# Rounding the next filter's weights at step 7 instead of 15, and building the attention bias ahead of the stores

## The chip, the cores and the metric

The kernel runs on one core of one Trainium2 chip. The metric is the device time of one execution in microseconds. The median of three runs before the change is 1096.94 us (1096.89 to 1097.17).

## The reference, cut to what matters

One layer of a hybrid encoder over 272 positions (256 tokens and 16 meta tokens) of width 2048. One input projection feeds three mixers, each gated, and their sum goes through an output projection:

```
z = rmsnorm(h) @ w_in                       # 2048 -> 16384 columns, split into the blocks below
u, x1, x2 = split(short_conv(hy_in))
kf  = rfft(filter from sin-MLP @ w4 * exp(-t * |decay|))     # hyena filter, 2 orders, two directions
y_a = hyena(u, x1, x2, kf) * silu(hy_gate)
y_b = real(fft2(fn_in)) * silu(fn_gate)
s   = q @ k.T * scale + bias(rpb) (masked) ; y_c = softmax(s) @ v * silu(na_gate)
m   = g_a * (y_a @ w_a) + g_b * (y_b @ w_b) + g_c * (y_c @ w_c)
out = rmsnorm(h + m @ w_out)[16:]
```

## The kernel before, in words

**Arithmetic.** Every float32 matrix product is made of three matmuls on split operands: a high part (the value rounded to the format that TensorE takes) and a low part (what is left). ScalarE makes the high part (`w_hi`, `act.split`, line 1016) and VectorE the low part by a subtraction (`w_lo`, `lo_part`, line 1359). GpSimd makes the low part of the filter weights `w4` for the first filter of chunks 1 to 3 (line 554).

**Chunks and steps.** The mixers' channels are cut into four chunks of 256 (`c` = 0 to 3). A chunk has 20 steps (`t`), and each step multiplies one slab of projection weights (48 matmuls, some 6 us) on TensorE. A block of columns takes two steps: u 0 and 1, q 2 and 3, k 4 and 5, v 6 and 7, x1 8 and 9, x2 10 and 11, the hyena gate 12 and 13, the Fourier input 14 and 15, then the other two gates. Between slabs TensorE does the mixers' smaller products. The slab of step `t + 2` is split during step `t`. A chunk takes 146 us, and the rows of chunks 0, 1 and 2 are 146.02 us apart to 0.02 us around the places in question.

**Order.** Each engine has its own list of instructions, written out by hand, in which a step's position is fixed; semaphores hold an instruction until its inputs are there. An engine never goes past an instruction that waits. What matters here:

- step 7, ScalarE and VectorE: after the softmax of head 0 (ScalarE's `soft`, VectorE's `normalized`, line 1709, which counts `p_done`) the first half of a slab is split, then VectorE copies block v out of PSUM (line 1595), which counts `proj_read`;
- step 8, TensorE: after its slab it turns the probabilities of head 0 (`turn_p`, lines 751 and 753, waits for `p_done`), and then v (`turn`, line 701, waits for `proj_read`);
- step 13, VectorE: the softmax of head 3. `biased` counts `smax_done` (line 1703), the slab is split, and `normalized` counts `p_done`;
- step 14, TensorE: after its slab, `attend(2)` and then `turn_p` of head 3, which waits for that `p_done`;
- step 15: ScalarE and VectorE finish the output of head 3 (`attended`, lines 1211 and 1721, `o_done`); TensorE's inverse transform waits for `o_done` at its second half (line 728, matmuls of line 717). VectorE's list has `fin_mirrors` (lines 1572 to 1574) ahead of `attended`.

**The filter.** `weights4(b)` on ScalarE rounds the weights `w4s` into `w4_hi` (line 1076) and takes the absolute value of `absd` (line 1078). When `w4_hi` is there, GpSimd subtracts to get `w4_lo` (line 554). The first user of the two is `make_h4` at step 16. GpSimd issues the loads of `w4s` and `absd` as soon as the filter before is no longer needed (`load_filter`, from step 2 on).

**GpSimd's list in a chunk:** load the next bias rows, load the next filter, `w4_lo`, store y_a, store y_c, load a filter, store y_b, and build the bias of the next chunk (`make_bias`: four additions of 128x384 at line 528, one for each head, and two copies at line 530).

Of the kernel before, what the change touches and what calls it, by code (L numbers as in the profile page):

```python
# [46 lines left out]
HC = HEADS // CH  # L47
# [146 lines left out]
def build(nc, x, meta, w_stream, filt_in, sym_in, fch_in, ftok_in, net_in, negt_in, mask_in, ident_in, params_in, w4,  # L194
# [138 lines left out]
    with ExitStack() as ctx:  # L333
        ps = ctx.enter_context(nc.psum_tensor("ps", [128, 8, 512], F32))

        def sem(name):
            return ctx.enter_context(nc.semaphore(name))
# [64 lines left out]
        smax_done = sem("smax_done")  # L402
# [72 lines left out]
        def _(pool):  # L475
# [9 lines left out]
            def load_filter(g):  # L485
                if g:
                    pool.wait_ge(h4_mm, 3 * g)
                    pool.wait_ge(env_done, 3 * g)
                for rows in (slice(0, HID), slice(HID, 2 * HID)):
                    pool.dma_start(w4s[rows, :, :].rearrange("p d n -> p (d n)"), w4[g]).then_inc(w4_landed, 16)  # L490
                pool.dma_start(absd[:, :, :].rearrange("p d n -> p (d n)"),
                               decay[g].partition_broadcast(128)).then_inc(dec_landed, 16)
# [20 lines left out]
            def load_bias_rows(c):  # L513
                for s in range(2):
                    src = bass.AP(rpb.tensor, c * (HC * RPB_R * RPB_C) + ((5 - s) * RPB_C + KW - GRID_W),
                                  [[1, GRID_W], [RPB_R * RPB_C, HC], [1, RPB_W]])
                    pool.dma_start(rows_t[64 * s:64 * s + 64, :, :], src).then_inc(b_landed, 16)
                pool.dma_start(meta_t[:, :], mbias[bass.ds(c, 1), :].rearrange("a n -> (a n)").partition_broadcast(128)
                               ).then_inc(b_landed, 16)

            def make_bias(c):
                pool.wait_ge(b_landed, (c + 1) * 48)
                for hh in range(HC):
                    grid = bias_t[:, hh, NM:NM + 6 * GRID_W].rearrange("p (j k) -> p j k", j=6)
                    flat = rows_t[:, hh, :]
                    toeplitz = bass.AP(flat.tensor, flat.offset, [[flat.ap[0][0], 128], [RPB_C, 6], [1, GRID_W]])
                    msk = mask[:, :].rearrange("p (a k) -> p a k", a=1).broadcast_to([128, 6, GRID_W])
                    nc.gpsimd.tensor_tensor(grid, toeplitz, msk, ALU.add)
                for lo in (0, NM + 6 * GRID_W):
                    last = nc.gpsimd.tensor_copy(bias_t[:, :, lo:lo + NM], meta_t[:, :].rearrange("p (h m) -> p h m", h=HC))  # L530
                last.then_inc(b_ready, 1)

            def store_y(c, branch, done):
                pool.wait_ge(done, c + 1)
                pool.dma_start(y_dram[branch, :, bass.ds(c * 2, 2), :], ystage[:, :, :]).then_inc(y_written, 16)
# [13 lines left out]
            for c in range(LAST):  # L549
                pool.wait_ge(b_ready, c + 1)  # L550
                load_bias_rows(c + 1)
                load_filter(2 * c + 2)
                pool.wait_ge(w4hi_done, 2 * c + 3)
                nc.gpsimd.tensor_tensor(w4_lo[:, :, :], w4s[:, :, :], w4_hi[:, :, :].bitcast(F32), ALU.subtract).then_inc(w4lo_done, 1)
                store_y(c, 0, ya_done)
                store_y(c, 2, yc_done)
                load_filter(2 * c + 3)
                store_y(c + 1, 1, yb_done)
                pool.wait_ge(smax_done, (c + 1) * HC)
                make_bias(c + 1)  # L560
            pool.wait_ge(n2_mm, CH)
            pool.wait_ge(h4_mm, 3 * NG_F)
            load_y(0, 16 * (3 * CH - 2))
# [23 lines left out]
        def _(pe):  # L587
# [243 lines left out]
            for c in range(CH):  # L831
                for t in range(S1):
                    name, _, n = BLOCKS[t // 2]
                    if t % 2 == 0:
                        pe.wait_ge(proj_read, 1 + c * NBLK + t // 2 - (c == LAST and name == "fgate"))
# [172 lines left out]
        def _(act):  # L1008
# [65 lines left out]
            def weights4(g):  # L1074
                act.wait_ge(w4_landed, 32 * g + 32)
                A(w4_hi[:, :, :], w4s[:, :, :], ACT.Copy).then_inc(w4hi_done, 1)
                act.wait_ge(dec_landed, 16 * g + 16)
                A(absd[:, :, :], absd[:, :, :], ACT.Abs).then_inc(dec_abs, 1)
                act.wait_ge(dec_abs, g + 1)
# [10 lines left out]
            def envelope(g, tt):  # L1090

                if g:
                    act.wait_ge(h4_read, 3 * g - 2 + tt)
                A(envel[:, tt, :, :], absd[:, :, :], ACT.Exp, scale=negt[:, tt:tt + 1]).then_inc(env_done, 1)

            def far_envelope(g):

                if g:
                    act.wait_ge(h4_read, 3 * g)
                c, o_ = divmod(g, 2)  # L1100
                for d in range(2):
                    for i in range(2):
                        at_ = DEC + 8 * (2 * o_ + d) + 2 * c + i
                        ins = A(far_env[:, d, i, :], negt[:, 2:2 + 2 * NM], ACT.Exp, scale=params[:, at_:at_ + 1])
                ins.then_inc(env_done, 1)

            def sd_high(g, tt):

                act.wait_ge(sd_done, 2 * g + tt + 1)
                A(sd_hi[:, tt, :, :], sd[:, :, :], ACT.Copy).then_inc(sdhi_done, 1)  # L1110

            def keep_x(g):
                c, o_ = divmod(g, 2)
                act.wait_ge(kx_mm, g + 1)
                if c:
                    act.wait_ge(y_full, 4 * c - 2 + 2 * o_)
                A(kspec[:, o_, 0, :, :].rearrange("p r n -> p (r n)"), ps[:, 7, :], ACT.Copy).then_inc(kx_evac, 1)

            def filter_step(c, t, place_):

                at_ = (t, place_)
                if c >= 0:
                    a = 2 * c + 1
                    if at_ == (0, 0 if c else 1):
                        keep_x(2 * c)
                    if at_ == (0, 1):
                        weights4(a)
                    if at_ == (1, 1):
                        envelope(a, 0)
                        envelope(a, 1)  # L1130
                    if at_ == (2, 0):
                        sd_high(a, 0)
                        far_envelope(a)
                    if at_ == (3, 0):
                        sd_high(a, 1)
                    if at_ == (4, 2):
                        keep_x(a)
                if c + 1 < CH:
                    b = 2 * c + 2
                    if at_ == (15, 1):  # L1140
                        weights4(b)
                    if at_ == (16, 1):
                        envelope(b, 0)
                        envelope(b, 1)
                    if at_ == (17, 0):
                        sd_high(b, 0)
                        far_envelope(b)
                    if at_ == (18, 0):
                        sd_high(b, 1)
# [118 lines left out]
            for c in range(0, CH):  # L1268
                for t in range(S1):
                    filter_step(c, t, 0)  # L1270
                    split(slab_of(c, t) + 2, 0)
                    filter_step(c, t, 1)
                    if t == 15:
                        attended(c, 3)
                        if c < LAST:
                            evac(c, "fin", 7)
                    split(slab_of(c, t) + 2, 1)
                    filter_step(c, t, 2)
                    if t in (3, 11):
                        turned(c * 3 + (1 if t == 3 else 3), t_hi, uT_hi[:, 0:2, :], uT_hi[:, 2, :], 4, t_mm)  # L1280
# [740 lines left out]
```

## Time and profile before

| quantity | value |
|---|---|
| median of three runs | 1096.94 us |
| the profiled execution | 1096.92 us |
| its span (first to last instruction) | 1095.1 us |
| TensorE (PE) busy | 1072.8 us, 98% of the span |
| VectorE (DVE) busy | 764.3 us, 70% |
| ScalarE (ACT) busy | 542.8 us, 50% |
| GpSimd (POOL) busy | 67.9 us, 6% |
| mean granted TensorE clock | 0.998 |

In the profile times are counted from the start of the span. A row of the view in order of time has the start, the duration in us, the engine, the line of the kernel, the operation, what it writes and reads, and how many instructions the row holds. In brackets stands idle time of the engine just before the row, with what ended it. A row's duration runs from its issue to its end, so what an instruction waits for inside the engine is part of it. Consecutive instructions of an engine overlap a little.

### The profile page before, as it was taken

The numbers are of one execution on the slowest core, as the hardware profiler recorded it, in microseconds if no ns is written. First come the engines' busy times: TensorE is split into PE (matmuls) and PEld (weight loads), VectorE is DVE, ScalarE is ACT, GpSimd is POOL, SyncE is SP. The second block draws the span as 40 slices with busy tenths as digits, with TensorE's granted clock in tenths as the row PEclk, the third lists the DMA queues.
The fourth block names the chain that finished last, engine by engine and source line by source line (L and its number), as shares of the span: only waits on it lengthen the run. The fifth ranks groups of instructions, "written<-read, shape, count | busy, mean of one in ns | idle before, by whom it ended". The sixth has DMA issues, their size and how long they took to land.

```text
span 1095.1 us, 16828 instructions
## 1 busy us (share of the span) xinstructions
PE 1072.8 (98%) x6944; PEld 982.1 (90%) x6944; DVE 764.3 (70%) x1158; ACT 542.8 (50%) x779; POOL 67.9 (6%) x104
## 2 busy tenths in 40 slices
PE   5999999999999999999999999999999999999997
PEld 5999999999999999999999888888888888888886
DVE  7877888697986888876888875544555545454654
ACT  6664564454545555545455454444444444444443
POOL 5120000300003000011000000000000000000000
PEclk9999999999999999999999999999999999999999
DMA  9764343644436544356434665555555555557552
GB/s 358 256 201 144 129 152 132 209 169 155 153 127 202 182 154 147 124 186 209 145 131 149 239 215 195 194 183 194 195 185 192 195 193 185 195 192 287 211 194 111
DMA packets 30748, 201.74 MB, mean 184 GB/s; under 512 B 3888, under 2 KB 4304, under 8 KB 7984
## 3 DMA queue, kind: packets, MB, share of 16 engines
q1 hardware_dynamic: 25264, 180.34, 47.8%
q0 software_dynamic: 5264, 19.80, 5.6%
q8 instruction: 55, 0.90, 0.3%
q10 hardware_dynamic: 144, 0.52, 0.1%
q14 instruction: 21, 0.17, 0.0%
HBM read 195.41 MB, written 5.24 MB: 183 GB/s over the span
## 4 chain that ended last, share of the span: by engine, by line
PE 94%; DVE 3%; ACT 1%; DMA 1%; issue 0%; SPq 0%; ACTq 0%
PE ps L591 29%; PE ps L593 29%; PE ps L592 29%; DVE w_lo L1359 1%; PE ps L701 1%; PE ps L751 1%; DMA xin<-x 1%; PE ps L596 1%; PE ps L717 0%; PE ps L634 0%; PE ps L743 0%; PE ps L742 0%; PE ps L635 0%; PE ps L646 0%; PE ps L753 0%; PE ps L958 0%
## 5 line engine op out<-in xcount | busy, mean ns | idle before, releaser
L1359 DVE TENSOR_TENSOR w_lo<-raw,w_hi 128x1024 fp32r<-128x1024 f32 (+1 forms) x338 | 411.4, 1232 | 246.6 <-ACT w_hi L1016 245.2
L1016 ACT ACTIVATE w_hi<-raw 128x1024 fp32r<-128x1024 f32 x334 | 348.8, 1056 | 351.6 <-PE ps L593 351.2
L591 PE MATMUL ps<-xn_hi,w_hi 128*128 128x272 f32 (+2 forms) x1280 | 368.5, 288 | 0.3 <-DVE xn_lo L1414 0.3
L593 PE MATMUL ps<-xn_hi,w_lo 128*128 128x272 f32 (+2 forms) x1280 | 364.7, 285 | 0.0
L592 PE MATMUL ps<-xn_lo,w_hi 128*128 128x272 f32 (+2 forms) x1280 | 364.5, 285 | 0.0
L591 PEld LDWEIGHTS ps<-xn_hi,w_hi 128*128 128x128 f32 x1280 | 241.2, 188 | 1.7 <-DVE xn_lo L1414 0.7
L592 PEld LDWEIGHTS ps<-xn_lo,w_hi 128*128 128x128 f32 x1280 | 241.2, 188 | 0.3
L593 PEld LDWEIGHTS ps<-xn_hi,w_lo 128*128 128x128 f32 x1280 | 241.2, 188 | 0.0
L591 PE MATMUL ps<-w_hi,xg_hi 128*128 128x512 f32 x352 | 137.2, 390 | 0.0
L593 PE MATMUL ps<-w_hi,xg_lo 128*128 128x512 f32 x352 | 137.0, 389 | 0.0
L592 PE MATMUL ps<-w_lo,xg_hi 128*128 128x512 f32 x352 | 136.9, 389 | 0.0
L593 PEld LDWEIGHTS ps<-w_hi,xg_lo 128*128 128x128 f32 x352 | 66.1, 188 | 13.8
L592 PEld LDWEIGHTS ps<-w_lo,xg_hi 128*128 128x128 f32 x352 | 66.1, 188 | 13.6
L591 PEld LDWEIGHTS ps<-w_hi,xg_hi 128*128 128x128 f32 x352 | 66.1, 188 | 13.6
L591 PE MATMUL ps<-w_hi,yb_hi 128*128 128x512 f32 x192 | 74.8, 389 | 0.0
L593 PE MATMUL ps<-w_hi,yb_lo 128*128 128x512 f32 x192 | 74.7, 389 | 0.0
L592 PE MATMUL ps<-w_lo,yb_hi 128*128 128x512 f32 x192 | 74.7, 389 | 0.0
L591 PE MATMUL ps<-w_hi,m_hi 128*128 128x512 f32 x128 | 49.9, 390 | 0.0
L593 PE MATMUL ps<-w_hi,m_lo 128*128 128x512 f32 x128 | 49.8, 389 | 0.0
L592 PE MATMUL ps<-w_lo,m_hi 128*128 128x512 f32 x128 | 49.8, 389 | 0.0
L591 PEld LDWEIGHTS ps<-w_hi,yb_hi 128*128 128x128 f32 x192 | 36.0, 188 | 7.7 <-issue 0.2
L593 PEld LDWEIGHTS ps<-w_hi,yb_lo 128*128 128x128 f32 x192 | 36.0, 188 | 7.5
(287 smaller groups left out, 1248.9 us busy)
## 6 DMA issues: line engine op xcount, KB each, us to landing
raw<-w_stream SPq DMA_DIRECT2D x167, 1024.0 KB, 4.9
branch_y<-ystage POOLq DMA_DIRECT2D x12, 256.0 KB, 4.0
y_raw<-branch_y POOLq DMA_DIRECT2D x3, 1024.0 KB, 7.1
xin<-x SPq DMA_DIRECT2D x2, 1024.0 KB, 6.0
w4s<-w POOLq DMA_DIRECT2D x16, 128.0 KB, 4.5
absd<-decay POOLq DMA_DIRECT2D x8, 256.0 KB, 5.0
h<-x POOLq DMA_DIRECT2D x2, 1024.0 KB, 8.3
rows_t<-rpb POOLq DMA_DIRECT2D x8, 219.0 KB, 5.9
```

The lines of the kernel that those rows point to most:

```text
L591: mm(out_ap, a_hi, b_hi, start=first, stop=False)
L592: mm(out_ap, a_hi, b_lo, start=False, stop=False)
L593: return mm(out_ap, a_lo, b_hi, start=False, stop=last)
L596: return mm(out_ap, a, b, start=first, stop=last)
L701: last = nc.tensor.transpose(dst, src[:, i, p:p + n], ident[:, :])
L751: nc.tensor.transpose(ps[:, 6, NG * kt + 128 * a:NG * kt + 128 * a + 128], sco[:, a, g0 + 128 * kt:g0 + 128 * kt + 128], ident[:, :])
L1016: A(w_hi[:, w % 2, part, :], raw[:, w % 4, 1024 * part:1024 * part + 1024], ACT.Copy).then_inc(hi_done, 1)
L1359: return V.tensor_tensor(dst, src, hi.bitcast(F32), ALU.subtract)
```

## The change

It changes two places: the step at which ScalarE executes `weights4` for the next chunk's first filter (chunks 0 to 2), and where in GpSimd's list `make_bias` stands, with the wait ahead of it.

```diff
@@ gpsimd, for c in range(LAST)
                 pool.wait_ge(w4hi_done, 2 * c + 3)
                 nc.gpsimd.tensor_tensor(w4_lo[:, :, :], w4s[:, :, :], w4_hi[:, :, :].bitcast(F32), ALU.subtract).then_inc(w4lo_done, 1)
+                pool.wait_ge(smax_done, (c + 1) * HC)
+                make_bias(c + 1)
                 store_y(c, 0, ya_done)
                 store_y(c, 2, yc_done)
                 load_filter(2 * c + 3)
                 store_y(c + 1, 1, yb_done)
-                pool.wait_ge(smax_done, (c + 1) * HC)
-                make_bias(c + 1)
@@ scalar, filter_step
-                    if at_ == (15, 1):
+                    if at_ == (7, 1):
                         weights4(b)
```

ScalarE's list at steps 6 to 8 of chunk 0 (`w_hi<-raw` are the slabs' splits, `sco` the softmax of head 0, `pT_hi` the turned probabilities):

```order
 L1016 ACTIVATE w_hi<-raw 128x1024 x2
 L1222 ACTIVATE sco,stat<-sco,stat 128x272 x2
-L1016 ACTIVATE w_hi<-raw 128x1024 x4
+L1016 ACTIVATE w_hi<-raw 128x1024
+L1076 ACTIVATE w_hi<-w4s 128x512
+L1078 ACTIVATE absd<-absd 128x512
+L1016 ACTIVATE w_hi<-raw 128x1024 x3
 L1193 ACTIVATE pT_hi<-ps 128x512
 L1194 ACTIVATE pT_rest<-ps 16x256
```

The two instructions of `weights4` stand behind the first of the four splits that follow the softmax. At step 15 they are gone from between the splits and `attended`:

```order
 L1195 ACTIVATE pT_rest<-ps 16x256
 L1016 ACTIVATE w_hi<-raw 128x1024 x3
-L1076 ACTIVATE w_hi<-w4s 128x512
-L1078 ACTIVATE absd<-absd 128x512
 L1211 ACTIVATE o<-ps 64x256
 L1180 ACTIVATE fi_hi<-fi 128x544
```

GpSimd's list in chunk 0 (`w_lo<-w4s,w_hi` is the filter weights' low part, `branch_y<-ystage` are the stores):

```order
 L491 DMA absd<-decay 128x512
 L554 TENSOR_TENSOR w_lo<-w4s,w_hi 128x512
+L528 TENSOR_TENSOR bias_t<-rows_t,mask 128x384 x4
+L530 COPY bias_t<-meta_t 128x4x16 x2
 L535 DMA branch_y<-ystage 128x512 x2
 L490 DMA w4s<-w 64x512 x2
 L491 DMA absd<-decay 128x512
 L535 DMA branch_y<-ystage 128x512
-L528 TENSOR_TENSOR bias_t<-rows_t,mask 128x384 x4
-L530 COPY bias_t<-meta_t 128x4x16 x2
```

The bias instructions pass three stores and one filter load; the wait for `smax_done` moves with them. The lists of TensorE, VectorE and SyncE are the same.

## Rows read from the trace of the kernel before

**Rows 1.** The page, part 1: busy time of TensorE.
```profile
PE 1072.8 (98%) x6944; PEld 982.1 (90%) x6944; DVE 764.3 (70%) x1158; ACT 542.8 (50%) x779; POOL 67.9 (6%) x104
```

**Rows 2.** TensorE's waits: total us, times, longest us.
```profile
PE ps L717 <- DVE o L1721: 3.7, 3, 1.2
```

**Rows 3.** In order of time, TensorE at step 15 of chunk 0.
```profile
168.16 0.39 PE L717 MATMUL ps<-sym_hi,y_hi 128*128 128x272 f32 x1 [1.23 <-DVE o L1721]
```

**Rows 4.** In order of time, VectorE, steps 14 and 15 of chunk 0.
```profile
163.60 1.22 DVE L1359 TENSOR_TENSOR w_lo<-raw,w_hi 128x1024 fp32r<-128x1024 f32 x1
164.74 2.31 DVE L1359 TENSOR_TENSOR w_lo<-raw,w_hi 128x1024 fp32r<-128x1024 f32 x1
...
167.68 0.42 DVE L1721 TENSOR_TENSOR o<-o,ps 64x256 f32<-64x256 f32 x1
```

**Rows 5.** In order of time, GpSimd at the same place.
```profile
164.24 1.73 POOL L554 TENSOR_TENSOR w_lo<-w4s,w_hi 128x512 fp32r<-128x512 f32 x1 [90.22 <-ACT w_hi L1076]
```

**Rows 6.** In order of time, ScalarE at the same place.
```profile
162.59 1.04 ACT L1016 ACTIVATE w_hi<-raw 128x1024 fp32r<-128x1024 f32 x1
163.53 0.61 ACT L1076 ACTIVATE w_hi<-w4s 128x512 fp32r<-128x512 f32 x1
...
165.66 0.38 ACT L1211 ACTIVATE o<-ps 64x256 f32<-64x256 f32 x1 [0.99 <-PE ps L763]
```

**Rows 7.** In order of time, ScalarE at step 7 of chunk 0.
```profile
108.81 1.04 ACT L1016 ACTIVATE w_hi<-raw 128x1024 fp32r<-128x1024 f32 x1
```

**Rows 8.** In order of time, VectorE at step 7 of chunk 0.
```profile
110.62 0.36 DVE L1709 TENSOR_SCALAR sco<-sco,stat 128x272 f32<-128x272 f32 x1
...
111.17 1.22 DVE L1359 TENSOR_TENSOR w_lo<-raw,w_hi 128x1024 fp32r<-128x1024 f32 x1
112.31 0.72 DVE L1595 COPY v<-ps 128x544 f32<-128x544 f32 x1
```

**Rows 9.** In order of time, TensorE behind the slab of step 8.
```profile
112.41 0.38 PE L751 MATMUL ps<-ident,sco 128*128 128x128 f32 x2
...
113.08 0.33 PE L701 MATMUL ps<-ident,v 128*128 128x128 f32 x1
```

**Rows 10.** In order of time, GpSimd's bias additions: chunk 0's, then chunk 1's four.
```profile
53.95 0.97 POOL L528 TENSOR_TENSOR bias_t<-rows_t,mask 128x384 f32<-128x384 f32 x1
...
55.84 1.95 POOL L528 TENSOR_TENSOR bias_t<-rows_t,mask 128x384 f32<-128x384 f32 x1
...
200.04 3.65 POOL L528 TENSOR_TENSOR bias_t<-rows_t,mask 128x384 f32<-128x384 f32 x4
```

**Rows 11.** In order of time, VectorE beside the first two of these.
```profile
54.05 1.02 DVE L1359 TENSOR_TENSOR y_lo<-fch_sum,y_hi 128x129 fp32r<-128x129 f32 x1
54.99 0.67 DVE L1631 SCALAR_TENSOR_TENSOR gate<-gate,ps 128x512 f32<-128x512 f32 x1
55.59 1.37 DVE L1359 TENSOR_TENSOR w_lo<-raw,w_hi 128x1024 fp32r<-128x1024 f32 x1
```

**Rows 12.** In order of time, VectorE at step 13 of chunk 0.
```profile
153.09 0.17 DVE L1703 TENSOR_SCALAR stat<-stat 128x2 f32<-128x2 f32 x1
153.16 0.68 DVE L1359 TENSOR_TENSOR y_lo<-prod,y_hi 128x512 fp32r<-128x512 f32 x1
153.97 1.22 DVE L1359 TENSOR_TENSOR w_lo<-raw,w_hi 128x1024 fp32r<-128x1024 f32 x1
155.11 1.22 DVE L1359 TENSOR_TENSOR w_lo<-raw,w_hi 128x1024 fp32r<-128x1024 f32 x1
...
156.60 0.63 DVE L1709 TENSOR_SCALAR sco<-sco,stat 128x272 f32<-128x272 f32 x2
```

**Rows 13.** In order of time, TensorE behind the slab of step 14.
```profile
158.09 0.38 PE L751 MATMUL ps<-ident,sco 128*128 128x128 f32 x2
```

**Rows 14.** In order of time, VectorE beside the last bias addition of chunk 1.
```profile
202.84 1.93 DVE L1359 TENSOR_TENSOR w_lo<-raw,w_hi 128x1024 fp32r<-128x1024 f32 x1 [3.66 <-ACT w_hi L1016]
```

**Rows 15.** In order of time, a long multiplication of VectorE at the start.
```profile
9.37 1.29 DVE L1428 TENSOR_SCALAR xin<-xin,stat 128x2048 f32<-128x2048 f32 x1
```

## The prediction

> **What bounds the kernel now.** I read the page first. TensorE is busy for 98% of the span [rows 1], so a change that adds no TensorE work can only win or lose in its gaps. The view of the waits comes next: behind the start-up there is one wait that repeats, the matmuls of line 717 for VectorE's `o` (line 1721), 3.7 us in 3 times, 1.2 each [rows 2]. Those are chunks 0, 1 and 2, the very chunks in which `weights4` runs at step 15. Then I read the engines in order of time around it. TensorE stands 1.23 us and starts at 168.16 [rows 3]; VectorE finished `o` at 167.68 + 0.42 = 168.10, so a semaphore takes 0.06 us from VectorE to TensorE. Two instructions earlier VectorE's list has two equal subtractions of 128x1024, of which one took 1.22 and the other 2.31 us [rows 4]. The longer one lies beside GpSimd's only subtraction of the chunk, 164.24 to 165.97 [rows 5].
>
> These rows fit one mechanism: GpSimd and VectorE take turns at something, one whole instruction at a time. GpSimd's additions of 128x384 take 3.65 / 4 = 0.91 us each [rows 10], so a subtraction of 128x512 is 0.91 x 512 / 384 = 1.22 us of work. Its row has 1.73: it waited 0.51, until 164.75, when VectorE's first subtraction was through (that row ends at 164.82, so VectorE lets go about 0.07 before a row ends). VectorE's second one was issued at 164.74, waited until GpSimd's end at 165.97, and ended at 167.05, 1.08 behind it (its 1.22 less 0.14 of issue). Chunk 0's bias shows the same over several turns: `y_lo` (54.05, 1.02 us) ended 0.15 after GpSimd's addition ended at 54.92; the next `w_lo` ended at 55.59 + 1.37 = 56.96; and GpSimd's addition issued at 55.84 took 1.95 in place of 0.91 [rows 10, 11]. So they alternate, also when one of them has several in a row. What reads PSUM isn't held: `gate` at 54.99 took 0.67 in the midst of it [rows 11].
>
> **Part 1, leaving step 15.** GpSimd's subtraction is gone from there, and VectorE's second `w_lo` takes 1.22 in place of 2.31: 1.09 us. Everything to `o` moves by that, since ScalarE's half of `o` is there at 165.66 + 0.38 = 166.04 [rows 6] and VectorE would want it at 167.68 - 1.09 = 166.59. `o` is done at 167.01, TensorE goes on at 167.07 in place of 168.16. What is late next is the same `o`, by 0.14 of the 1.23. The 1.1 us that ScalarE gets back there are worth nothing by themselves, as ScalarE then waits for TensorE anyway (0.99 before `o`) [rows 6]. Gain: 1.09 us a chunk.
>
> **Part 2, arriving at step 7.** ScalarE's split of 108.81 [rows 7] ends at 109.85. At step 15 the weights' rounding was issued 0.10 before the end of the split ahead of it, took 0.61, and GpSimd started 0.10 after its end [rows 5, 6]. Here that gives 109.75, 110.36, and 110.46 for GpSimd. VectorE's next instruction is the pair at line 1709, issued at 110.62 [rows 8], so GpSimd comes first and holds until 110.46 + 1.22 = 111.68. If the pair is held like `w_lo`, its first ends at 111.68 + 0.36 - 0.14 = 111.90 in place of 110.98: 0.92 late, say 0.9. The pair is through at 112.15, in time for `turn_p` at 112.41 [rows 9]. Behind it stand `w_lo` and the copy of v, issued at 112.31, that ended at 113.03 [rows 8]; with the semaphore that is 113.09, and TensorE turned v at 113.08 [rows 9]. There is no slack at all. The copy comes 0.9 late, and so does TensorE. ScalarE's two instructions push its three splits by 1.1 us; VectorE uses them only after the copy of v, which is late by 0.9 itself, so I cost this at nothing; without that cover it would be up to 0.2 of `w_lo` work behind v, for slabs that TensorE takes up a step later. Loss: 0.9 us a chunk.
>
> **Part 3, the bias at step 13.** `smax_done` of head 3 is counted at 153.26 [rows 12], so four additions and two copies start there, where VectorE has `y_lo`, two `w_lo` and the pair of head 3 in a row. By turns, with a hand-over 0.07 before a VectorE row's end and a VectorE row ending 0.14 less than its own time after GpSimd's end:
>
> - `y_lo` ends at 153.84, GpSimd's 1st runs 153.77 to 154.68
> - `w_lo` ends at 155.76 (was 155.19); 2nd to 156.60
> - `w_lo` ends at 157.68 (was 156.33, so 1.35 late); 3rd to 158.52
> - the pair's first would be issued at 156.60 + 1.35 = 157.95, ends at 158.74; 4th to 159.58
> - the pair's second ends at 159.79, in place of 156.60 + 0.63 = 157.23 [rows 12]
>
> TensorE wants that pair for `turn_p` at 158.09 [rows 13] and gets it at 159.79 + 0.06 = 159.85. Its slack was 0.80, the delay is 2.56: loss 1.76 us a chunk. ScalarE's and VectorE's work of steps 14 and 15 follows `turn_p` and moves along with it, so part 1's gain stays as it is. At the old place the bias held a `w_lo` at 202.84 for 0.71 us (1.93 less 1.22) [rows 14]; VectorE had idled 3.66 us before it and no wait of TensorE falls there, so getting this back gives nothing. The stores behind the bias aren't late: the first one waits for y_a, which VectorE makes only behind step 15's inverse transform, later than 168. The next loads of bias rows, behind the stores, come earlier by the time of `make_bias`, which nobody waits for.
>
> **Sum.** 3 x (-1.09 + 0.9 + 1.76) = 3 x 1.57 = +4.7 us. From the profiled execution's 1096.92 us (span 1095.1; it is 0.02 below the median of 1096.94) that makes 1101.6 us.
>
> **The unknown cost.** No row shows the pair, a multiplication with one input in SBUF, beside a GpSimd instruction. The nearest rows lie at both ends: `w_lo` and `y_lo` (two inputs in SBUF) are held for the whole GpSimd instruction, `gate` (one of its inputs in PSUM) not at all. Held not at all: step 7 costs 111.68 + 1.08 = 112.76 against 111.17 + 1.22 = 112.39, so 0.37; at step 13 the pair ends at 157.68 + 0.90 = 158.58, a loss of 0.55; sum 3 x (-1.09 + 0.37 + 0.55) = -0.5. Held for more than a turn: if GpSimd keeps its place through all it has in hand, it is done at 153.77 + 3.65 + 2 x 0.23 (a copy's time, taken as a quarter of an addition) = 157.88, the `w_lo` end at 158.96 and 160.10, the pair at 161.00, a loss of 2.97 and +8.3 in sum. Below nothing I find only the case without parts 2 and 3, -3.3. I take the held end with turns, because of the speed of such multiplications: 2048 elements in 1.29 us [rows 15] is 1.6 per ns, twice the 0.84 of `w_lo` (1024 in 1.22), so it draws on at least as much of VectorE's path to SBUF as `w_lo` with its two inputs does.
>
> The Trainium skill weighs in on this: "SBUF — State Buffer", section "Who interferes with whom", says that VectorE and GpSimd share a pair of SBUF ports under an exclusive lock, and that a `tensor_scalar` that moves two elements a cycle takes that pair just as an instruction with two SBUF inputs does. By that the sum is +4.7, without it -0.5. The trace agrees as far as the doubled speed goes; the collision itself no run here shows.
>
> **Rivals.**
>
> - *The pair is not held.* For it: no row shows it held. Against it: its speed. Both collisions lose most of their price: 1096.92 - 0.5 = 1096.4 us.
> - *The pair passes in one go between GpSimd's 3rd and 4th addition.* For it: its two halves are issued 0.28 apart, closer than the others. Against it: in [rows 10, 11] each gap between two additions let exactly one VectorE instruction through, a short `y_lo` as well as a long `w_lo`. Pair through at 158.52 + 0.22 + 0.27 = 159.01, loss 0.98, sum 3 x 0.79 = +2.4: 1099.3 us.
> - *GpSimd doesn't give way between its instructions.* For it: nothing. Against it: the alternation in [rows 10, 11]. 1105.2 us.
> - *Faster: the wait at step 15 goes and no other comes.* It decides on the slack of v at step 7 and of the pair at step 13. If GpSimd's subtraction finds VectorE busy or comes after the copy of v, and the bias starts later than the two `w_lo` (GpSimd takes over 2.3 us from `smax_done` to its start, when its rows show 0.1 behind a semaphore), only part 1 is left: 1096.92 - 3.3 = 1093.6 us. For it: TensorE's gap is certain to shrink, and GpSimd's start is a matter of tenths. Against it: no slack at v, 0.8 us at the pair, and 4.1 us of GpSimd work put right there.
>
> **How the numbers follow.** Forecast with turns 0.50, in one go 0.15, no giving way 0.07, pair not held 0.15, only the gain 0.13. A measurement of this kernel can tell about 0.2%, 2.2 us, from no change. Slower by more: 0.50 + 0.15 + 0.07 = 0.72; within: 0.15; faster: 0.13. The likeliest case has its own range of 1099 to 1103.3. The whole range reaches down to the case of no change, 1096.0, and up to 1103.3; it leaves out the faster case and the one without giving way, 0.20.
>
> **What would show it.** Right: the wait of line 717 falls from 1.2 to some 0.1 us, three times; new waits of TensorE of 0.9 us at line 701 for v (line 1595) and of 1.8 us at line 751 for `sco` (line 1709), three each; VectorE's pair at step 7 begins with an instruction of some 1.3 us in place of 0.36; the two `w_lo` at step 13 last about 1.8 to 2.0; GpSimd's additions there 1.4 to 1.9 each. Wrong: rows of line 1709 still at 0.36 beside GpSimd (then 1096.4), or GpSimd's subtraction starting later than VectorE's pair at step 7, or the wait of line 717 unchanged, which would say that it wasn't GpSimd that stretched the `w_lo`.

## The result

| | median, us | span of the profiled execution |
|---|---|---|
| before | 1097.10 (1096.89 to 1097.26, 5 runs) | 1095.1 |
| changed | 1101.38 (1101.04 to 1101.64, 5 runs) | 1099.3 |

The ratio is 1.0038, with a 95% interval of 1.0027 to 1.0049: slower by 4.3 us. The profiled execution of the changed kernel took 1101.10 us, 4.2 more than that of before.

TensorE's waits in the changed kernel (total us, times, longest us), which answer to [rows 2]:

```profile
PE ps L751 <- DVE sco L1709: 4.0, 3, 1.3
...
PE ps L701 <- DVE v L1595: 2.4, 3, 0.8
```

The wait of line 717 for `o` is gone from this list. In its place stand two others, three times each: one wait a chunk was traded for two, and it is VectorE that TensorE waits for each time. The rows below are those of chunk 0; chunks 1 and 2 repeat them.

**Step 7.** The changed kernel in order of time, GpSimd:

```profile
110.36 1.29 POOL L554 TENSOR_TENSOR w_lo<-w4s,w_hi 128x512 fp32r<-128x512 f32 x1 [36.45 <-ACT w_hi L1076]
```

VectorE beside it, in the changed kernel (to [rows 8]):

```profile
110.51 1.30 DVE L1709 TENSOR_SCALAR sco<-sco,stat 128x272 f32<-128x272 f32 x1
111.74 0.35 DVE L1709 TENSOR_SCALAR sco<-sco,stat 128x272 f32<-128x272 f32 x1
112.01 1.21 DVE L1359 TENSOR_TENSOR w_lo<-raw,w_hi 128x1024 fp32r<-128x1024 f32 x1
113.14 0.71 DVE L1595 COPY v<-ps 128x544 f32<-128x544 f32 x1
```

TensorE in the kernel before, the last instruction of `turn_p`, which stands just ahead of the v of [rows 9]:

```profile
112.96 0.27 PE L753 MATMUL ps<-ident,sco 128*16 128x128 f32 x1
```

The same instruction and the first of v in the changed kernel:

```profile
112.85 0.27 PE L753 MATMUL ps<-ident,sco 128*16 128x128 f32 x1
113.91 0.33 PE L701 MATMUL ps<-ident,v 128*128 128x128 f32 x1 [0.79 <-DVE v L1595]
```

VectorE's first instruction of the pair took 1.30 us in place of 0.36, because GpSimd's subtraction was issued 0.15 ahead of it: it ended 111.81 - 111.65 = 0.16 behind GpSimd. Before, v was turned 113.08 - 112.96 = 0.12 behind `turn_p`; now it is 113.91 - 112.85 = 1.06: TensorE loses 0.94 us.

**Steps 13 and 14.** The changed kernel in order of time, GpSimd's four additions:

```profile
154.18 1.33 POOL L528 TENSOR_TENSOR bias_t<-rows_t,mask 128x384 f32<-128x384 f32 x1 [42.52 <-DVE stat L1703]
155.46 1.91 POOL L528 TENSOR_TENSOR bias_t<-rows_t,mask 128x384 f32<-128x384 f32 x1
157.34 1.92 POOL L528 TENSOR_TENSOR bias_t<-rows_t,mask 128x384 f32<-128x384 f32 x1
159.22 1.01 POOL L528 TENSOR_TENSOR bias_t<-rows_t,mask 128x384 f32<-128x384 f32 x1
```

VectorE beside them, in the changed kernel (to [rows 12]):

```profile
153.93 0.17 DVE L1703 TENSOR_SCALAR stat<-stat 128x2 f32<-128x2 f32 x1
154.00 0.69 DVE L1359 TENSOR_TENSOR y_lo<-prod,y_hi 128x512 fp32r<-128x512 f32 x1
154.81 1.78 DVE L1359 TENSOR_TENSOR w_lo<-raw,w_hi 128x1024 fp32r<-128x1024 f32 x1
156.51 1.95 DVE L1359 TENSOR_TENSOR w_lo<-raw,w_hi 128x1024 fp32r<-128x1024 f32 x1
...
158.57 0.85 DVE L1709 TENSOR_SCALAR sco<-sco,stat 128x272 f32<-128x272 f32 x1
159.34 1.05 DVE L1709 TENSOR_SCALAR sco<-sco,stat 128x272 f32<-128x272 f32 x1
```

TensorE in the kernel before, the last instruction ahead of the `turn_p` of [rows 13] and the one behind its first row:

```profile
157.96 0.29 PE L763 MATMUL ps<-pT_lo,v_two 128*128 128x256 f32 x1
...
158.31 0.27 PE L753 MATMUL ps<-ident,sco 128*16 128x128 f32 x1
```

The same three rows in the changed kernel:

```profile
158.81 0.29 PE L763 MATMUL ps<-pT_lo,v_two 128*128 128x256 f32 x1
160.44 0.44 PE L751 MATMUL ps<-ident,sco 128*128 128x128 f32 x2 [1.35 <-DVE sco L1709]
160.72 0.27 PE L753 MATMUL ps<-ident,sco 128*16 128x128 f32 x1
```

GpSimd's additions and the instructions of VectorE that are held take turns, one of each. The two `w_lo` end at 156.59 and 158.46, 1.08 and 1.09 us behind the end of an addition, as at step 15 before. The two halves of the pair end at 159.42 and 160.39, each 0.16 behind one. The additions end 0.78 to 0.82 behind VectorE's end. A short reciprocal of VectorE with one input isn't held (158.38, 0.15 us). `turn_p` came 158.09 - 157.96 = 0.13 behind the instruction of line 763 and now comes 1.63 behind it, a loss of 1.50 us. Its first two matmuls then take 160.72 - 160.44 = 0.28 us in place of 158.31 - 158.09 = 0.22, so that 1.56 us are lost here.

**Step 15.** The changed kernel in order of time, VectorE (to [rows 4]):

```profile
166.00 1.22 DVE L1359 TENSOR_TENSOR w_lo<-raw,w_hi 128x1024 fp32r<-128x1024 f32 x1
167.15 1.22 DVE L1359 TENSOR_TENSOR w_lo<-raw,w_hi 128x1024 fp32r<-128x1024 f32 x1
...
168.99 0.42 DVE L1721 TENSOR_TENSOR o<-o,ps 64x256 f32<-64x256 f32 x1
```

TensorE in the kernel before, the instruction ahead of that of [rows 3]:

```profile
166.71 0.22 PE L718 MATMUL ps<-sym_hi,y_lo 128*128 128x136 f32 x1
```

The same instruction and the one behind it in the changed kernel:

```profile
169.12 0.22 PE L718 MATMUL ps<-sym_hi,y_lo 128*128 128x136 f32 x1
169.47 0.39 PE L717 MATMUL ps<-sym_hi,y_hi 128*128 128x272 f32 x1
```

Both `w_lo` take 1.22. From the one to the other TensorE took 168.16 - 166.71 = 1.45 us before and takes 0.35 now: 1.10 back. In all 3 x (0.94 + 1.56 - 1.10) = 4.2 us, as many as lie between the two profiled executions. The chunks agree: GpSimd's first addition starts at 154.18, 301.64 and 449.09 in the changed kernel, 147.46 and 147.45 us apart, 1.44 more than the 146.02 of before.

### The profile page after: what moved, and what is told of

It is laid out like the page before. It is cut to its first block, busy times and chain, and to the rows that moved or that the text cites. A ratio compares the mean times of both kernels' runs of the same rounds, so it can differ in the third digit from the quotient of the medians.

```text
span 1099.3 us, 16825 instructions
## 1 busy us (share of the span) xinstructions
PE 1073.8 (98%) x6944; PEld 982.0 (89%) x6944; DVE 769.5 (70%) x1158; ACT 542.7 (49%) x779; POOL 70.8 (6%) x104
## 4 chain that ended last, share of the span: by engine, by line
PE 87%; DVE 9%; ACT 2%; issue 1%; DMA 1%; SPq 0%; ACTq 0%; DVEq 0%
PE ps L591 27%; PE ps L592 27%; PE ps L593 27%; DVE w_lo L1359 3%; DVE sco L1709 1%; PE ps L701 1%; DMA xin<-x 1%; PE ps L717 1%; DVE x L1604 0%; PE ps L751 0%; PE ps L634 0%; PE ps L596 0%; DVE far_y L1518 0%; DVE prod L1647 0%; DVE pT_lo L1359 0%
```

## The experiments

All but the last were timed against the kernel before. Each edit is against the kernel before unless it says otherwise.

**1. The rounding at step 7 alone.**

```diff
-                    if at_ == (15, 1):
+                    if at_ == (7, 1):
                         weights4(b)
```

> The rounding of the next filter's weights at step 7 as in the change, the bias at its old place behind the stores. Turn-taking (GpSimd and VectorE exclude each other for one whole instruction): step 15 gives back 1.10 us a chunk, TensorE's new wait for v at step 8 costs 0.94, nothing else: 3 x -0.16 = -0.5, so 1096.6 us, no change that can be told, with the wait of line 701 at 0.8 to 0.9 and none at line 751. Rival (the loss at v comes from ScalarE's two added instructions or from the bias): the time would be 1093.8 or the wait at line 701 would be missing.

Measured 1096.71 us against 1097.11, ratio 0.9996 (0.9987 to 1.0005). TensorE's waits, the start-up's rows left out:

```profile
PE ps L701 <- DVE v L1595: 2.4, 3, 0.8
```

This half is a trade of 1.10 for 0.94 a chunk, and can't be told from no change. The wait for v comes with it, without the bias, and there is none at line 751.

**2. The bias at step 13 alone,** ahead of GpSimd's subtraction, which stays at step 15.

```diff
+                pool.wait_ge(smax_done, (c + 1) * HC)
+                make_bias(c + 1)
                 pool.wait_ge(w4hi_done, 2 * c + 3)
                 nc.gpsimd.tensor_tensor(w4_lo[:, :, :], ...)
...
                 store_y(c + 1, 1, yb_done)
-                pool.wait_ge(smax_done, (c + 1) * HC)
-                make_bias(c + 1)
```

> The kernel before, with the bias built at step 13, ahead of GpSimd's wait for the rounded weights; the rounding stays at step 15. Turn-taking: only the loss at the pair of head 3, 3 x 1.50 = +4.5: 1101.6 us; the wait of line 717 stays at 1.2 and a wait of 1.3 at line 751 comes. Rival (the two parts of the change work on each other, for instance TensorE's wait at step 8 makes the one at step 14 shorter or longer): the time would be off 1101.6 by 1 us or more.

Measured 1101.87 us, ratio 1.0044 (1.0032 to 1.0057). TensorE's waits:

```profile
PE ps L751 <- DVE sco L1709: 4.0, 3, 1.3
...
PE ps L717 <- DVE o L1721: 3.7, 3, 1.2
```

This half carries the whole slowdown, +4.8 us, nearer to 3 x 1.56 = 4.7 than to the 4.5 expected. The two halves sum to -0.4 + 4.8 = +4.4 us, and the change measured +4.3. Each half's waits are also those of the changed kernel, so no effect of one on the other is to be seen, though with these intervals one of about 1 us could hide in the times.

**3. The rounding behind the softmax of head 3 (step 13).**

```diff
-                    if at_ == (15, 1):
-                        weights4(b)
...
                     if t in (9, 11, 13):
                         soft(c, (t - 7) // 2)
+                    if t == 13 and c < LAST:
+                        weights4(2 * c + 2)
```

> The kernel before, with the rounding of the next filter's weights moved from step 15 to step 13, behind ScalarE's exponentials of head 3; bias at its old place. There VectorE has only the pair under way and then one instruction that reads PSUM and 2.8 us of idle time. Turn-taking: GpSimd's subtraction runs from 157.2 to 158.4 beside nothing that it holds, step 15 gives its 1.10 us a chunk: 1097.1 - 3.3 = 1093.8 us, faster than both. Rival (the gain of step 15 is tied to ScalarE's list and not to GpSimd): also 1093.8, so this alone doesn't tell them; it tells whether a collision comes back: a wait at line 751 would mean that GpSimd got in ahead of the pair, 1096 us or more.

Measured 1093.78 us, ratio 0.9970 (0.9959 to 0.9981): faster than both kernels. GpSimd in this kernel, in order of time:

```profile
157.35 1.41 POOL L554 TENSOR_TENSOR w_lo<-w4s,w_hi 128x512 fp32r<-128x512 f32 x1 [82.99 <-ACT w_hi L1076]
```

VectorE beside it:

```profile
157.25 0.36 DVE L1709 TENSOR_SCALAR sco<-sco,stat 128x272 f32<-128x272 f32 x1
157.53 0.68 DVE L1631 SCALAR_TENSOR_TENSOR gate<-gate,ps 128x512 f32<-128x512 f32 x1
161.07 0.69 DVE L1359 TENSOR_TENSOR pT_lo<-ps,pT_hi 128x512 fp32r<-128x512 f32 x1 [2.86 <-ACT pT_rest L1193]
```

GpSimd came 0.10 behind the pair's second half and waited for it (1.41 in place of the 1.29 of step 7). The `gate` beside it, which has an input in PSUM, wasn't touched, and behind it VectorE is idle. TensorE has no wait at line 751, and that of line 717 is down to 0.3 us in 2 times, 0.2 at the longest.

**4. The changed kernel with the copy of v ahead of the split.** The edit is against the changed kernel.

```diff
+                    if t == 7:
+                        evac(c, "v", 3)
                     split(slab_of(c, t) + 2, 0)
...
-                    if t == 7:
-                        evac(c, "v", 3)
                     split(slab_of(c, t) + 2, 1)
```

> The changed kernel, with VectorE's copy of v at step 7 ahead of the split of the slab's first half in place of behind it. If the loss at step 8 is that v has no slack behind a held pair, the wait of line 701 goes; the slab's low part, now behind the copy, is ready at 113.92 where TensorE would want it at 113.60, so 0.3 of the 0.94 stays: 3 x -0.62, 1101.4 - 1.9 = 1099.5 us. Rival (TensorE is late at step 8 through ScalarE's later splits): the time stays at 1101.4.

Measured 1099.51 us (1098.85 to 1099.90), ratio to the kernel before 1.0021 (1.0012 to 1.0030), as expected. TensorE waits for the slab's low part instead (waits of its weight loads, same columns):

```profile
PEld ps L591 <- DVE w_lo L1359: 1.2, 3, 0.4
```

So the loss at step 8 comes from v standing last in VectorE's delayed list. That ScalarE's later splits have no part in it is shown by the next experiment.

**5. ScalarE moved, GpSimd not.** The rounding at step 7, GpSimd's subtraction held until step 15, where it was.

```diff
-                    if at_ == (15, 1):
+                    if at_ == (7, 1):
...
                 pool.wait_ge(w4hi_done, 2 * c + 3)
+                pool.wait_ge(hi_done, 2 * (slab_of(c, 15) + 2) + 1)
                 nc.gpsimd.tensor_tensor(w4_lo[:, :, :], ...)
```

> ScalarE rounds the weights at step 7 as in the change, but GpSimd's subtraction is held back to step 15 by a wait for ScalarE's first split there, so that it lies beside VectorE's second w_lo as before; bias at its old place. If it was GpSimd's instruction and not ScalarE's two that made TensorE wait at line 717: the wait stays at 1.2, none comes at line 701, 1097.1 us. Rival (ScalarE's two instructions delayed its half of o): 1093.8 us.

Measured 1097.13 us, ratio 0.9999 (0.9990 to 1.0008). TensorE's waits (the lines stand one higher here):

```profile
PE ps L718 <- DVE o L1722: 3.7, 3, 1.2
```

GpSimd at step 15, and VectorE's second `w_lo` beside it:

```profile
164.35 2.19 POOL L555 TENSOR_TENSOR w_lo<-w4s,w_hi 128x512 fp32r<-128x512 f32 x1 [89.78 <-ACT w_hi L1017]
165.31 2.31 DVE L1360 TENSOR_TENSOR w_lo<-raw,w_hi 128x1024 fp32r<-128x1024 f32 x1
```

This separates what the change moves together. ScalarE's 1.1 us are gone from step 15 and nothing is won; they stand at step 7, where the pair takes 0.63 us for both halves as before, and no wait for v comes. Both waits are GpSimd's doing.

**6. The bias moved as in the change, the rounding not.**

```diff
                 nc.gpsimd.tensor_tensor(w4_lo[:, :, :], ...)
+                pool.wait_ge(smax_done, (c + 1) * HC)
+                make_bias(c + 1)
                 store_y(c, 0, ya_done)
...
-                pool.wait_ge(smax_done, (c + 1) * HC)
-                make_bias(c + 1)
```

> The change's second half alone: the bias ahead of the stores and behind the subtraction, which stays at step 15 with the rounding. The bias then starts at step 15 (some 167 us in chunk 0). Turn-taking: a w_lo and the low part of the Fourier input are held, 1.3 us together, ahead of the unfolding that TensorE waits for at step 16 (line 634, 0.3 us before): 3 x 1.3 = +3.9, 1101.0 us, with the wait of line 717 still 1.2. Rival (beside step 15 and 16 the bias is free, as at step 20): 1097.1.

Measured 1100.61 us, ratio 1.0032 (1.0019 to 1.0046). This is a collision at yet another place, priced ahead of the run by the same rule: +3.9 us expected, +3.5 measured. Beside the additions a `w_lo` took 1.62 us in place of 1.21 and the Fourier input's low part 1.48 in place of 0.72, together 1.17 where 1.3 was expected. TensorE's waits:

```profile
PE ps L717 <- DVE o L1721: 3.7, 3, 1.2
PE ps L634 <- DVE u L1685: 3.6, 3, 1.2
```

**7. The rounding at the end of step 6.**

```diff
-                    if at_ == (15, 1):
+                    if at_ == (6, 2):
                         weights4(b)
```

> The kernel before, with the rounding moved to the end of step 6, ahead of the softmax of head 0, where VectorE is idle for 3.45 us behind two w_lo; bias at its old place. Turn-taking: the second w_lo is 1.2 us late, into the idle time; step 15 gives its 1.10: 1093.8 us, no wait at lines 701 and 751. Rival (the early rounding costs something wherever it stands): 1096 or more.

Measured 1093.68 us, ratio 0.9968 (0.9956 to 0.9981). VectorE, whose idle time was 3.45 us at this place:

```profile
101.77 2.31 DVE L1359 TENSOR_TENSOR w_lo<-raw,w_hi 128x1024 fp32r<-128x1024 f32 x1
106.44 0.06 DVE L1697 MEMSET stat<- 128x1 f32 x1 [2.36 <-PE ps L743]
```

Here the collision still happens, with the same 2.31 us as at step 15, and costs nothing, because 2.36 us of idle time follow it. TensorE has none of the waits at lines 701, 717 and 751. Experiments 3 and 7 can't be told from each other; both beat both kernels.

**8. Memsets in the bias's place,** one profiled execution, against the changed kernel.

```diff
             def make_bias(c):
                 pool.wait_ge(b_landed, (c + 1) * 48)
-                for hh in range(HC):
+                for n in range(4 if c else 0):
+                    nc.gpsimd.memset(bias_t[:, :, :].rearrange("p h n -> p (h n)"), 0.0).then_inc(pool_link, 1)
+                    pool.wait_ge(pool_link, 4 * (c - 1) + n + 1)
+                for hh in range(0 if c else HC):
```

> The changed kernel, with each of the later chunks' bias (four additions and two copies of GpSimd, which read and write SBUF) left out and four memsets of the whole bias tile in its place, one behind the other, which only write; the bias of chunks 1 to 3 is therefore zero. One look at what it is that excludes. If a GpSimd instruction that only writes excludes all of VectorE's SBUF work: both w_lo of step 13 last 1.8 to 2.6 us as beside the additions. If, as the Trainium skill says (SBUF, Who interferes with whom), two inputs collide only with GpSimd's reads and a doubled-speed instruction with anything: w_lo 1.22 us, and the pair of line 1709 over 0.6 each as long as a memset is under way. Third: nothing is held, and TensorE's wait at line 751 is gone.

The copies for the meta tokens were still executed behind the memsets, so what the kernel leaves out is the bias of the grid in chunks 1 to 3. The execution took 1101.88 us. In order of time, GpSimd's first and third memset:

```profile
154.66 1.50 POOL L524 MEMSET bias_t<- 128x1664 f32 x1 [42.49 <-DVE stat L1706]
...
157.77 1.49 POOL L524 MEMSET bias_t<- 128x1664 f32 x1
```

VectorE beside the memsets (its lines stand three higher here):

```profile
155.32 1.23 DVE L1362 TENSOR_TENSOR w_lo<-raw,w_hi 128x1024 fp32r<-128x1024 f32 x1
156.46 1.22 DVE L1362 TENSOR_TENSOR w_lo<-raw,w_hi 128x1024 fp32r<-128x1024 f32 x1
...
157.95 1.46 DVE L1712 TENSOR_SCALAR sco<-sco,stat 128x272 f32<-128x272 f32 x1
159.33 1.66 DVE L1712 TENSOR_SCALAR sco<-sco,stat 128x272 f32<-128x272 f32 x1
```

TensorE's `turn_p` behind it:

```profile
161.04 0.44 PE L754 MATMUL ps<-ident,sco 128*128 128x128 f32 x2 [1.44 <-DVE sco L1712]
```

Beside a GpSimd instruction that only writes, `w_lo` with its two inputs runs as if alone, and each half of the pair is held nearly through a whole memset. So the two kinds of VectorE instruction are held by different things: `w_lo` by additions, which also read SBUF, but not by memsets, and the multiplication, which the prediction took from [rows 15] to run at doubled speed, by both. The Trainium skill, "SBUF — State Buffer", section "Who interferes with whom", says that two SBUF inputs collide only with a GpSimd instruction that reads SBUF, and an instruction in a doubled-speed mode that uses both port pairs with any. The rows agree.

## Why the prediction was right

It said 1101.6 us and 1101.38 was measured. The mechanism and the three terms held; that the two times lie within 0.3 us is in part luck, since the sum was 0.4 us above the measured difference, and the kernel before came out at 1097.10, 0.2 above the 1096.92 that the sum started from. By its parts, per chunk:

| part | predicted | profile | tested by |
|---|---|---|---|
| 1, leaving step 15 | -1.09 | -1.10 | 5 (GpSimd's, not ScalarE's), 3 and 7 |
| 2, arriving at step 7 | +0.9 | +0.94 | 1 and 4 |
| 3, bias at step 13 | +1.76 | +1.56 | 2, and 6 at another place |
| sum of three chunks | +4.7 | +4.2 | change measured +4.3 |

*Part 1.* `w_lo` fell from 2.31 to 1.22 and the wait of line 717 to its remainder: the matmul starts 169.47 - 169.34 = 0.13 us behind the end of the row ahead, where 0.14 was forecast, and `o` is still what it waits for (168.99 + 0.42 + 0.06 = 169.47). The weight loads show 0.3 at most for it. ScalarE's two instructions were costed at nothing, and experiment 5 shows no cost.

*Part 2.* GpSimd was forecast at 110.46 against the pair at 110.62, and came at 110.36 against 110.51: the order on which the term hung held by 0.15 us. The first of the pair took 1.30, and the copy of v had no slack, as said.

*Part 3.* The turns came in the order listed. The size was 0.20 too high: the pair's delay was 0.24 too long, and the 0.06 by which the first matmuls were slower stand against that. The pair's second half ended at 159.34 + 1.05 = 160.39; from `smax_done`, which is counted 0.84 later than before, that is 2.32 late, and I had 2.56. Each hand-over was a little quicker than the two figures taken from step 15: the third addition ended 0.10 earlier than listed, the fourth 0.19, and each half of the pair ended 0.16 behind GpSimd where I had 0.22. The list of signs asked for additions of 1.4 to 1.9 us each, which doesn't follow from the prediction's own turns: the first and the fourth took 1.33 and 1.01, as each waited for one short VectorE instruction only. The view of the waits shows 0.8 and 1.3 us at lines 701 and 751 where the signs had 0.9 and 1.8, and where 0.94 and 1.50 were lost: it counts from the end of the row ahead, and TensorE's rows overlap.

*The slack given back at the bias's old place.* There `w_lo` fell from 1.93 to 1.23 us [rows 14], with the same 3.66 us of idle time ahead of it, and TensorE has no wait there before or after: worth nothing, as said.

*The rivals.* The pair not held: refuted by its 1.30, 0.85 and 1.05 us. In one go: refuted, as GpSimd's fourth addition lies between the halves. GpSimd not giving way: refuted by the same rows. Only the gain: this is what experiments 3 and 7 have, 3.3 and 3.5 us below the kernel before, when the subtraction is put where it holds nothing that TensorE waits for.

The three places account for 4.2 of the 4.3 us. The 0.1 that is left is within what these runs can tell.

## What to carry to other kernels

A GpSimd instruction of a microsecond is no background work, however little of the span GpSimd is busy: ask which VectorE instructions stand beside it, and how much slack the last of them has before TensorE wants its result. When such work is moved, price the place it arrives at as closely as the one it leaves, with the collisions in turns, and choose a place where VectorE is idle next or reads PSUM. A train of GpSimd instructions weighs most on short VectorE instructions in a row, since each waits for a turn of its own: the pair's 0.36 us became 0.85 and 1.05.

## What the runs showed of the hardware that the prediction did not use

Whether VectorE is held depends on what GpSimd's instruction does. Beside memsets the two `w_lo` took 1.23 and 1.22 us, as alone; beside additions 1.78 and 1.95. The 128x272 multiplication, 0.36 alone, took 1.46 and 1.66 beside memsets of 1.5. The four memsets cost TensorE about as much as the additions (1.44 us at that wait against 1.35), though they hold only the pair: each is 1.5 us long where an addition is 0.91.
